# Norm statistics taken while tiles arrive, softmax in PSUM, and a layer loop written out: a two-part network on one core

## The chip, the core and the metric

The kernel runs on one core of a Trainium2 chip. The metric is the device time of one execution in microseconds. Five engines run their own instruction streams and wait for each other through semaphores: PE (matrix multiply; its weight loads are shown apart as PEld), DVE (vector), ACT (activation functions), POOL and SP, which here only issues the weight DMAs. SBUF is the working memory of 128 partitions; PSUM has eight banks of 128 x 512 float32, into which PE writes.

## The reference, cut to what matters

A sequence of 512 tokens of width 1024 goes through two layers of a first kind and then through two layers of a second kind.

```python
# first kind, twice (depth 2)
h = x @ w_in                                    # q, k, v of three attentions, gates
merged = g0*(fox(h)@w_up_fox) + g1*(stick(h)@w_up_sb) + g2*(sparse(h)@w_up_dsa)
x = layer_norm(ALPHA*x + merged @ w_out)        # "norm 1"
ffn = square(relu(x @ w_ff_in)) @ w_ff_out
ple = sigmoid(x @ w_ple_gate) * (p @ w_ple)
x = layer_norm(ALPHA*x + ffn + ple)             # "norm 2"
# layer_norm: (x - mean) * rsqrt(var + eps) * g + b, over the 1024 features

# second kind, twice
h = rms_norm(x); proj = h @ w_in_2
# compressed, selected and windowed attention (8 heads; q and k through rope tables)
pc = softmax(q @ kc + mask);  o_c = pc @ vc     # kc, vc: 31 compressed blocks
# gated linear recurrence: log_a = lam*(1+tanh(..)), a = exp(log_a),
#   h = scan(a, sqrt(1-a^2)*(i*xc))
# convolution branch: GLU, 31 taps, layer norm over 512 features, silu, @ w_pw2
x = x + concat(o*silu(z), h*silu(z), conv*silu(z)) @ w_out
# at the end: rms_norm(x)
```

## The kernel before

Activations lie feature-major: a tile is 128 features x 512 tokens, and x has eight of them (`KT = 8`). All products are done in float32 with three matmuls: every operand is cut into a high and a low part (`x_hi`, `x_lo`, `w_hi`, `w_lo`), and high x high, low x high and high x low are summed in PSUM (lines 397 to 399 in `pe_tile`). A weight unit is 128 x 1024 floats; a dense unit (`pe_unit`) is 8 tiles x 3 = 24 matmuls into one bank. Weights stream through four slots: SP loads `w_raw`, ACT makes `w_hi` (L406, after the slot's former unit was used), POOL makes `w_lo` (L423), and only then can PE use the unit. So each unit costs one ACT and one POOL instruction, and the order in which ACT comes to them is part of its program.

There is no scheduler. Each engine's program is written out by hand, and the order in it is the order of the code; waits are on semaphore counts. `pe_group` runs four units: the first two side by side, tile by tile as `x_ready` counts up (`pe_two_units`), then the others one after the other.

A layer norm of the first kind works in five steps over eight tiles: PE sums the tiles with a matrix of 1/1024 (L796), one tile behind the unit that makes it; when all eight are summed, DVE subtracts the mean (L837); ACT squares each tile (L820, two work tiles in turn) and PE sums the squares (L810); ACT takes the root (L822), DVE the reciprocal (L839); DVE multiplies (L843), ACT writes `x_hi` and a float32 copy with scale and bias (L826), DVE writes `x_lo` (L847), which counts `x_ready`. Behind norm 1, PE runs the two PLE units (four products of `p` each into banks 0 to 3), ACT copies each unit's four banks out (L1155) and then frees them together, and the FFN begins. Behind the very last norm 2, DVE adds `x_hi` and `x_lo` into `residual` (L1928), ACT squares it (L1395), PE sums (L1387), and root (L1400), reciprocal (L1414), scaling (L1418) and the split (L1407, L1423) follow.

Each layer of the second kind runs on DVE in this order: norm, rope tables from the positions (nine instructions, `b_rope_tables`), a small polynomial (`b_softplus`), gates and the 31-tap convolution (L1949 to L1967), the gate of the heads (L1981, on which PE's second rope matmul L1534 waits), rope and the block splits, the log decay (L2028), squares of `a` (L2068), the recurrence's factor (L2071), compressed keys and values into place (L2076, L2082), the scan (L2090), the compressed softmax (L2099 to L2119), the split of the convolution's output (L2122), and the copy of the compressed output (L2129). PE meanwhile runs dense units, the scores of the compressed attention (L1656), two more dense units, then the turned softmax weights (L1667), the product with the compressed values (L1675), two `pw2` units, and then the 64 steps of windowed and selected attention in two halves (`attn_pe`: scores L491, turn L501, output L520).

Both layer kinds are hardware loops over `DEPTH` on every engine, and the two attention halves are a loop too.

Of the kernel before, what the change touches and what calls it, by code (L numbers as in the profile page):

```python
# [24 lines left out]
P = 128  # L25
SEQ = 512
# [76 lines left out]
def plan(nc, ctx):  # L103
# [62 lines left out]
    S.eps = small("ln_eps", 1)  # L166

# [2225 lines left out]
```

## Time and profile before

| | |
|---|---|
| Median of three runs | 3076.24 us (3069.5, 3076.24, 3076.39) |
| Profiled execution | 3074.71 us, span 3072.9 us, mean granted clock 0.96 |
| PE busy | 2834.2 us (92%) |
| PE weight loads | 2209.6 us (72%) |
| DVE, ACT, POOL busy | 1564.3, 1171.7, 1069.9 us |
| DMA | 220.57 MB, mean 72 GB/s |

The span runs from the first to the last instruction. A busy share says how long an engine ran, not whether something waited for it; what counts is the idle time of the engine that bounds the span, and what ended it. The clock is that granted to PE: 1.00 is 2.4 GHz and 0.50 is 1.2 GHz; the mean over a stretch mixes the two.

### The profile page before, as it was taken

Reading aid. Unit: us, or ns where it says so; the run is one execution under the profiler, and the core shown is the slowest. Engines: PE = TensorE matmul, PEld = TensorE weight load, DVE = VectorE, ACT = ScalarE, POOL = GpSimd, SP = SyncE. Lnnn points to the kernel's source line nnn. Section 1 sums busy time; section 2 is a strip of 40 time slices with the busy share of each in tenths; the row PEclk is TensorE's granted clock in tenths of the full one; section 3 lists DMA queues with packets and bytes.
Section 4 is the critical chain, followed back from the end, with each engine's and each line's share of the span. In section 5 each row is a group of like instructions: output and inputs, shape, how many; then the busy total and the mean of one; then the engine's idle time right before and its main releaser. Section 6 shows DMA issues by size and latency. Waiting matters only on the chain. (4 is left out here: it accounts for less than half of the span.)

```text
span 3072.9 us, 39249 instructions
## 1 busy us (share of the span) xinstructions
PE 2834.2 (92%) x12850; PEld 2209.6 (72%) x12860; DVE 1564.3 (51%) x2745; ACT 1171.7 (38%) x1921; POOL 1069.9 (35%) x430
## 2 busy tenths in 40 slices
PE   7989899999999899998998999997996998998798
PEld 6857666678888687676766888865875776876676
DVE  2077536453232304764455223327898555889554
ACT  2344434243222433443424323235344443355343
POOL 3422112344444343111133445442464212455312
PEclk9999999999999999999999999998997999999899
DMA  4311111223233122111121232221231001222101
GB/s 151 102 49 49 37 40 55 76 72 99 90 103 101 59 93 82 36 48 42 36 87 58 94 102 96 96 82 49 98 114 62 28 31 56 96 96 96 35 28 48
DMA packets 61043, 220.57 MB, mean 72 GB/s; under 512 B 6896, under 2 KB 7024, under 8 KB 60784
## 3 DMA queue, kind: packets, MB, share of 16 engines
q1 hardware_dynamic: 60192, 217.12, 21.4%
q10 hardware_dynamic: 720, 1.84, 0.2%
q8 instruction: 66, 1.08, 0.2%
q14 instruction: 65, 0.53, 0.1%
HBM read 216.83 MB, written 2.10 MB: 71 GB/s over the span
## 5 line engine op out<-in xcount | busy, mean ns | idle before, releaser
L423 POOL TENSOR_TENSOR w_lo<-w_raw,w_hi 128x1024 fp32r<-128x1024 f32 x404 | 1018.1, 2528 | 1965.1 <-ACT w_hi L406 1950.7
L397 PE MATMUL bank<-x_hi,w_hi 128*128 128x512 f32 (+1 forms) x2160 | 915.1, 424 | 50.3 <-DVE x_lo L2194 17.7
L398 PE MATMUL bank<-x_lo,w_hi 128*128 128x512 f32 (+1 forms) x2160 | 855.5, 396 | 0.0
L399 PE MATMUL bank<-x_hi,w_lo 128*128 128x512 f32 (+1 forms) x2160 | 854.9, 396 | 0.0
L406 ACT ACTIVATE w_hi<-w_raw 128x1024 fp32r<-128x1024 f32 x400 | 419.3, 1054 | 542.0 <-PE bank L399 527.4
L397 PEld LDWEIGHTS bank<-x_hi,w_hi 128*128 128x128 f32 x2160 | 415.9, 193 | 170.4 <-issue 76.6
L399 PEld LDWEIGHTS bank<-x_hi,w_lo 128*128 128x128 f32 x2160 | 413.6, 191 | 90.1
L398 PEld LDWEIGHTS bank<-x_lo,w_hi 128*128 128x128 f32 x2160 | 416.0, 193 | 86.6 <-issue 13.8
L397 PE MATMUL bank<-rhs_hi,w_hi 128*128 128x512 f32 (+1 forms) x656 | 262.3, 400 | 4.2 <-DVE rhs_lo L1288 4.2
L398 PE MATMUL bank<-rhs_lo,w_hi 128*128 128x512 f32 (+1 forms) x656 | 255.5, 390 | 0.0
L399 PE MATMUL bank<-rhs_hi,w_lo 128*128 128x512 f32 (+1 forms) x656 | 255.3, 389 | 0.0
L543 ACT ACTIVATE work<-bank,neg_max 128x128 f32<-128x128 f32 x216 | 114.0, 528 | 288.5 <-DVE neg_max L564 285.4
L564 DVE TENSOR_REDUCE neg_max<-bank 128x1 f32<-128x128 f32 x216 | 105.3, 490 | 166.3 <-PE bank L491 138.0
L1353 DVE TENSOR_TENSOR ffn_sum<-ffn_sum,bank 128x512 f32 x64 | 43.9, 688 | 286.1 <-PE bank L399 286.1
L1343 DVE TENSOR_TENSOR work<-work 128x512 f32<-128x512 f32 x64 | 102.7, 1604 | 169.5 <-ACT rhs_hi L1170 169.5
L1967 DVE SCALAR_TENSOR_TENSOR bank<-glu_out,params_b_cur,bank 128x512 f32<-128x512 f32 x216 | 152.7, 753 | 34.0 <-issue 34.0
L397 PEld LDWEIGHTS bank<-rhs_hi,w_hi 128*128 128x128 f32 (+1 forms) x656 | 122.9, 187 | 50.9 <-issue 27.8
L1213 DVE TENSOR_SCALAR proj<-proj 128x1024 f32<-128x1024 f32 (+2 forms) x8 | 9.3, 1229 | 267.8 <-ACT proj L1032 267.8
L399 PEld LDWEIGHTS bank<-rhs_hi,w_lo 128*128 128x128 f32 (+1 forms) x656 | 123.0, 188 | 25.9
L398 PEld LDWEIGHTS bank<-rhs_lo,w_hi 128*128 128x128 f32 (+1 forms) x656 | 123.1, 188 | 23.2
L1168 ACT ACTIVATE work<-bank 128x512 f32<-128x512 f32 x64 | 38.0, 594 | 216.4 <-PE bank L399 216.4
L501 PE MATMUL bank<-constants,work 128*128 128x128 f32 x540 | 100.7, 285 | 18.0 <-ACT work L543 17.5
(387 smaller groups left out, 3688.2 us busy)
## 6 DMA issues: line engine op xcount, KB each, us to landing
w_raw<-w SPq DMA_DIRECT2D x404, 512.0 KB, 3.3
ln_in<-x SPq DMA_DIRECT2D x1, 2048.0 KB, 8.1
out<-residual SPq DMA_DIRECT2D x8, 256.0 KB, 2.2
p_raw<-p ACTq DMA_DIRECT2D x2, 512.0 KB, 3.5
positions<-pos ACTq DMA_DIRECT2D x2, 256.0 KB, 3.3
constants<-con SPq DMA_DIRECT2D x1, 455.0 KB, 3.2
cos<-cos SPq DMA_DIRECT2D x1, 256.0 KB, 3.4
sin<-sin SPq DMA_DIRECT2D x1, 256.0 KB, 3.7
```

Source lines behind the costliest of these rows:

```text
L397: nc.tensor.matmul(out, wh, xh, start=first, stop=False)
L398: nc.tensor.matmul(out, wh, xl, start=False, stop=False)
L399: S.last = nc.tensor.matmul(out, wl, xh, start=False, stop=last)
L406: S.nc.scalar.activation(S.wh[s][:, :], S.raw[s][:, :], ACT.Copy).then_inc(S.hi_ready[s], 1)
L423: S.nc.gpsimd.tensor_tensor(S.wl[s][:, :], S.raw[s][:, :], S.wh[s][:, :].bitcast(F32), ALU.subtract).then_inc(S.lo_ready[s], 1)
L501: m = nc.tensor.transpose(o[:, k * P:(k + 1) * P], S.wk[4 + n % 2][:, k * P:(k + 1) * P], ident)
L543: nc.scalar.activation(S.wk[4 + n % 2][:, 0:w], S.X[n % 2][:, 0:w], ACT.Exp, bias=S.nm[n % 4][:, :], accum_out=S.rs[n % 4][:, :]).then_inc ...
L564: nc.vector.tensor_reduce(S.nm[n % 4][:, :], S.X[n % 2][:, 0:w], AX, ALU.max, negate=True).then_inc(Z.max, 1)
L1168: nc.scalar.activation(S.wk[j % 2][:, :], S.ps[s][:, :], ACT.Relu).then_inc(S.bank_free[s], 1)
L1343: nc.vector.tensor_tensor(h, S.wk[j % 2][:, :], S.wk[j % 2][:, :], ALU.mult)
L1353: nc.vector.tensor_tensor(y, y, S.ps[s][:, :], ALU.add).then_inc(S.bank_free[s], 1)
L1967: stt(out=S.X[t % 2][:, :], in0=S.uc[:, bass.ds(i * 3 + (k + t * UC_W), SEQ)], scalar=S.curB[:, bass.ds(i * 3 + (k + PB_DW + t * CONV_K), ...
```

## The change

The norms of the first kind (`ln_*`) subtract twice X[0] from each tile as it comes (X[0] is a 1024th of the sum over the first four tiles, so twice it is their own mean), and square and sum the result at once; tiles 4 to 7 are also summed into X[2], which is the offset that is left. The variance is the sum of squares less the offset squared. The offset is taken out between the multiplications. The last of these norms writes `residual` and its square straight away. The root's table is called for by a dummy activation ahead of it. PLE banks are freed one by one, and the first group behind a norm runs three units side by side.

```diff
+def pe_side_by_side(S, pe, us, g, rh, rl, ready, n0, banks=None, free=None):
+
     for k in range(KT):
         pe.wait_ge(ready, n0 + k + 1)
-        for s in slots:
+        for u in us:
+            s = u % SLOTS
             if k == 0:
                 pe.wait_ge(S.lo_ready[s], g + 1)
                 pe.wait_ge(S.bank_free[s], banks[s] if banks else g + 1)
+                if free:
+                    free(s)
             pe_tile(S, s, k, S.ps[s][:, :], rh, rl, k, k == 0, k == KT - 1)
...
+def pe_group(S, pe, u0, g, rh, rl, ready, n0, banks=None, wide=2, free=None):
+
+    pe_side_by_side(S, pe, range(u0, u0 + wide), g, rh, rl, ready, n0, banks, free)
+    for u in range(u0 + wide, u0 + SLOTS):
...
+def ln_units_pe(S, pe, n0, t_sem, t0, t, unit):
+
+    def first_mean(j):
         pe.wait_ge(t_sem, t0 + j + 1)
-        return S.nc.tensor.matmul(S.X[0][:, :], S.ones[:, :], seq(t, j), start=(j == 0), stop=(j == KT - 1))
-
-    for j in range(SLOTS):
-        unit(j)
-        if 4 * i + j >= 1:
-            mean(4 * i + j - 1)
-    if i == 1:
-        mean(KT - 1).then_inc(S.ln_mean, 1)
-
-
-def ln_pe(S, pe, n0):
-
-    for j in range(KT):
-        pe.wait_ge(S.ln_sq, n0 * KT + j + 1)
-        S.nc.tensor.matmul(S.X[1][:, :], S.ones[:, :], S.wk[j % 2][:, :], start=(j == 0),
-                           stop=(j == KT - 1)).then_inc(S.ln_var, 1)
+        return S.nc.tensor.matmul(S.X[0][:, :], S.ones[:, :], seq(t, j), start=(j == 0), stop=(j == 3))
+
+    for x in range(KT):
+        unit(x)
+        if 1 <= x <= 4:
+            m = first_mean(x - 1)
+            if x == 4:
+                m.then_inc(S.ln_mean, 1)
+        if x == 6:
+            for j in range(4):
+                ln_square_pe(S, pe, n0, j)
+            for j in (4, 5):
+                ln_offset_pe(S, pe, n0, t, j)
+    for j in (4, 5, 6):
+        ln_square_pe(S, pe, n0, j)
+    for j in (6, 7):
+        ln_offset_pe(S, pe, n0, t, j)
+    ln_square_pe(S, pe, n0, 7)
...
+def ln_root_act(S, act, n0, t):
+
+    S.nc.scalar.activation(S.spare[:, :], S.eps[:, :], ACT.Sqrt)
+    ln_square_act(S, act, n0, t, 7)
+    act.wait_ge(S.ln_off, n0 + 1)
+    S.nc.scalar.activation(S.wk[0][:, :], S.X[2][:, :], ACT.Square).then_inc(S.ln_offsq, 1)
+    act.wait_ge(S.ln_v, n0 + 1)
+    S.nc.scalar.activation(S.wk[2][:, :], S.wk[1][:, :], ACT.Sqrt, bias=S.eps[:, :]).then_inc(S.norm_std, 1)
...
+def ln_last_act(S, act, n0, t, g, b):
...
+        S.nc.scalar.activation(S.wk[4 + j % 4][:, :], seq(t, j), ACT.Square, scale=scale, bias=bias).then_inc(S.norm_sq, 1)
+        S.nc.scalar.activation(seq(S.res, j), seq(t, j), ACT.Identity, scale=scale, bias=bias)
...
+def ln_less_first_dve(S, dve, n0, t, x):
+
+    if x == 4:
+        dve.wait_ge(S.ln_mean, n0 + 1)
+    for j in range(0 if x == 4 else x, x + 1):
+        if x >= 4:
+            S.nc.vector.scalar_tensor_tensor(out=seq(t, j), in0=S.X[0][:, :], scalar=-2.0, in1=seq(t, j), op0=ALU.mult,
+                                             op1=ALU.add).then_inc(S.ln_d, 1)
...
+def ln_dve(S, dve, n0, t, last=False):
     nc = S.nc
-    tiles = [t[:, j * SEQ:(j + 1) * SEQ] for j in range(KT)]
-    dve.wait_ge(S.ln_mean, n0 + 1)
-    for j in range(KT):
-        nc.vector.tensor_tensor(tiles[j], tiles[j], S.X[0][:, :], ALU.subtract).then_inc(S.ln_d, 1)
-    dve.wait_ge(S.ln_std, n0 + 1)
-    nc.vector.reciprocal(S.wk[3][:, :], S.wk[2][:, :])
+    tiles = [seq(t, j) for j in range(KT)]
+    dve.wait_ge(S.ln_offsq, n0 + 1)
+    dve.wait_ge(S.norm_var, n0 * KT + KT)
+    nc.vector.tensor_tensor(S.wk[1][:, :], S.X[1][:, :], S.wk[0][:, :], ALU.subtract).then_inc(S.ln_v, 1)
+
+    def center(j):
+        nc.vector.tensor_tensor(tiles[j], tiles[j], S.X[2][:, :], ALU.subtract)
+
+    center(0)
+    dve.wait_ge(S.norm_std, n0 + 1)
+    nc.vector.reciprocal(S.X[3][:, :], S.wk[2][:, :])
     dve.drain()
     for j in range(KT + 2):
         if j < KT:
-            nc.vector.tensor_tensor(tiles[j], tiles[j], S.wk[3][:, :], ALU.mult).then_inc(S.ln_y, 1)
-        if j >= 2:
+            nc.vector.tensor_tensor(tiles[j], tiles[j], S.X[3][:, :], ALU.mult).then_inc(S.norm_y, 1)
+        if j + 1 < KT:
+            center(j + 1)
+        if j >= 2 and not last:
             q = j - 2
-            dve.wait_ge(S.ln_hi, n0 * KT + q + 1)
+            dve.wait_ge(S.norm_hi, n0 * KT + q + 1)
             nc.vector.tensor_tensor(seq(S.xl, q), S.wk[4 + q % 4][:, :], seq(S.xh, q).bitcast(F32),
                                     ALU.subtract).then_inc(S.x_ready, 1)
+        dve.drain()
```

In the last layer of the first kind ACT loads the positions, and DVE makes the rope tables once, between the second and third quarter of the FFN; ACT takes the sines after the third. In the layers of the second kind they are no longer made.

```diff
+        if L == DEPTH - 1:
+            act.dma_start(S.prmB[:, :], T["prm_b"]).then_inc(S.pb_landed, 16)
+            act.dma_start(S.pos[:, :], T["pos"].to_broadcast([P, SEQ])).then_inc(S.pb_landed, 16)
+        with act.Fori(0, 3) as q:
+            ffn(q)
+        if L == DEPTH - 1:
+            act.wait_ge(S.ang_ready, 1)
+            nc.scalar.activation(S.sin[:, :], S.tab[2][:, :], ACT.Sin)
...
+        with dve.Fori(0, 2) as q:
+            ffn(q)
+        if L == DEPTH - 1:
+            b_rope_tables(S, dve)
...
-        b_rope_tables(S, dve, L)
```

The log decay and the squares of `a` go from DVE to ACT, the compressed softmax works in PSUM, the `pw2` units stand ahead of it on PE (their input has its own place, `un_hi` and `un_lo`), and its outputs go to four banks and are copied by two engines. The loops over the layers and over the attention halves are written out on every engine; inside a layer of the first kind the loops over the projections and the FFN stay.

```diff
+        for t in range(4):
+            lam = S.curB[:, PB_LAM + t:PB_LAM + t + 1]
+            nc.scalar.activation(seq(S.la, t), seq(S.la, t), ACT.Identity, scale=lam, bias=lam)
...
+        squared = (S.X[0], S.X[1], S.wk[2], S.wk[3])
+        for t in range(4):
+            nc.scalar.activation(squared[t][:, :], seq(S.la, t), ACT.Square).then_inc(S.a_ready, 1)
+        for t in range(4):
+            nc.scalar.activation(seq(S.unh, t), seq(S.cacc, t), ACT.Copy).then_inc(S.cl_hi, 1)
...
+            nc.vector.tensor_tensor(seq(S.unl, t), seq(S.cacc, t), seq(S.unh, t).bitcast(F32), ALU.subtract).then_inc(S.un_ready, 1)
...
-            p3 = S.wk[4 + h][:, :].rearrange("p (r n) -> p r n", n=32)
-            mx = S.cmx[:, 16 * h:16 * h + 16]
+            p3 = S.X[h][:, :].rearrange("p (r n) -> p r n", n=32)
+            mx = S.cmx[h]
+            nc.vector.tensor_tensor(p4, p4, mask, ALU.add)
...
+        for b in (1, 3):
+            act.wait_ge(S.oc_ready, L * 4 + b + 1)
+            nc.scalar.activation(S.ot2[:, b * 512:(b + 1) * 512], S.X[b][:, :], ACT.Copy).then_inc(S.oc_done, 1)
...
-    with pe.Fori(0, DEPTH) as L:
+    for L in range(DEPTH):
...
-        with pe.Fori(0, 2) as i:
-            pe.wait_ge(S.lru_done, L + 1)
-            pe.wait_ge(S.oc_done, L * 4 + 4)
-            pe.wait_ge(S.mc_y, L * 4 + 4)
+        pe.wait_ge(S.oc_done, L * 4 + 4)
+        for i in range(2):
```

On PE, at the end of norm 1: `merged` is the last output unit, `ln_in` a tile of the norm, `work` a squared tile, `p_hi` the first PLE unit. Before:

```order
L399 MATMUL bank<-merged_hi,w_lo_58 128x512
L796 MATMUL bank<-ln_in,ones 128x512 x2
L809 ISA
L810 MATMUL bank<-work_93,ones 128x512
L809 REGISTER_ALU
L810 MATMUL bank<-work_94,ones 128x512
```

And of the change:

```order
L404 MATMUL bank<-merged_hi,w_lo_58 128x512
L828 MATMUL bank<-work_93,ones 128x512
L828 MATMUL bank<-work_94,ones 128x512
L828 MATMUL bank<-work_95,ones 128x512
L834 MATMUL bank<-ln_in,ones 128x512 x2
L828 MATMUL bank<-work_96,ones 128x512
L402 MATMUL bank<-p_hi,w_hi_55 128x512
```

Behind the last unit there stood one mean matmul and eight squares; now there stand four squares and two offset matmuls, and six of their kind stand between the last two units.

On PE, at the compressed attention: `work` turned are its softmax weights, `un` the convolution's output for `pw2`. Before:

```order
L399 MATMUL bank<-x_hi,w_lo_58 128x512
L1667 MATMUL bank<-constants,work_97 128x128 x4
L1667 MATMUL bank<-constants,work_98 128x128 x4
L1675 MATMUL bank<-cmp_values,work_99 128x256 x4
L1675 MATMUL bank<-cmp_values,work_100 128x256 x4
L1440 REGISTER_ALU
L397 MATMUL bank<-x_hi,w_hi_55 128x512
```

And of the change:

```order
L404 MATMUL bank<-un_hi,w_lo_60 128x512
L1831 MATMUL bank<-constants,work_95 128x128 x4
L1831 MATMUL bank<-constants,work_96 128x128 x4
L1837 MATMUL bank<-cmp_values,work_99 128x256 x4
L1837 MATMUL bank<-cmp_values,work_100 128x256 x4
L496 MATMUL bank<-b_ks,work_93 128x128
```

The two `pw2` units moved ahead of the turned weights; the attention's first scores stand right behind the compressed output.

On DVE, from the factor of the recurrence to the softmax's first half. Before:

```order
L2068 TENSOR_TENSOR work_100<-lru_log_a 128x512
L2071 SCALAR_TENSOR_TENSOR lru_tmp<-work_97,lru_tmp 128x512
L2071 SCALAR_TENSOR_TENSOR lru_tmp<-work_98,lru_tmp 128x512
L2071 SCALAR_TENSOR_TENSOR lru_tmp<-work_99,lru_tmp 128x512
L2071 SCALAR_TENSOR_TENSOR lru_tmp<-work_100,lru_tmp 128x512
L2074 ISA
L2076 COPY cmp_keys<-bank 64x31 x2
L2082 COPY cmp_values<-bank 32x64 x8
L2087 SCALAR_TENSOR_TENSOR lru_i<-lru_i,lru_tmp 128x2048
L2090 TENSOR_TENSOR_SCAN lru_tmp<-lru_log_a,lru_i 128x512 x4
L2099 TENSOR_TENSOR work_97<-bank,cmp_mask 128x512
```

And of the change:

```order
L2194 SCALAR_TENSOR_TENSOR lru_tmp<-bank,lru_tmp 128x512 x2
L2194 SCALAR_TENSOR_TENSOR lru_tmp<-work_95,lru_tmp 128x512
L2194 SCALAR_TENSOR_TENSOR lru_tmp<-work_96,lru_tmp 128x512
L2199 COPY cmp_keys<-bank 64x31 x2
L2205 COPY cmp_values<-bank 32x64 x8
L2210 TENSOR_TENSOR un_lo<-conv_sum,un_hi 128x512 x4
L2214 MEMSET work_93 64x512
L2214 MEMSET work_94 64x512
L2219 SCALAR_TENSOR_TENSOR lru_i<-lru_i,lru_tmp 128x2048
L2222 SCALAR_TENSOR_TENSOR lru_tmp<-lru_log_a,lru_i 128x512 x4
L2231 TENSOR_TENSOR bank<-bank,cmp_mask 128x512
```

The four squares left DVE, the scan's row now reads as L2222, and four subtractions and two memsets that stood behind the softmax came ahead of the scan.

## Rows read from the trace of the kernel before

**Rows 1.** Waits of PE, longest first: total us, times, longest.

```profile
PE bank L1675 <- DVE b_o_tok L2129: 19.3, 2, 9.7
PE bank L1667 <- DVE work L2119: 18.9, 4, 8.9
PE bank L1387 <- ACT work L1395: 18.6, 1, 18.6
PE bank L397 <- ACT ple_proj L1155: 17.6, 4, 4.6
PE bank L501 <- ACT work L543: 17.5, 16, 4.2
PE bank L397 <- DVE x_lo L1423: 16.0, 2, 8.8
...
PE bank L1656 <- DVE cmp_keys L2076: 8.0, 2, 4.0
...
PE bank L1534 <- DVE b_gate_tok L1981: 7.2, 2, 3.6
```

**Rows 2.** Busy time by stretch, with clock: norms, first FFN units, compressed attention.

```profile
core 0: us, PE busy (x) PEld busy (x) DVE busy (x) ACT busy (x) POOL busy (x), PEclk, DMA share, GB/s
594.90:628.70 33.80, 22.65 (x69) 13.01 (x67) 22.13 (x28) 24.60 (x37) 5.13 (x2) 0.94 0.11 39
628.70:653.70 25.00, 24.96 (x97) 20.43 (x98) 16.15 (x7) 7.01 (x10) 10.51 (x4) 0.88 0.19 64
1028.90:1050.80 21.90, 11.38 (x21) 3.52 (x19) 12.44 (x16) 11.00 (x16) 2.86 (x1) 0.86 0.14 47
2058.10:2105.30 47.20, 18.34 (x37) 6.43 (x35) 31.84 (x52) 28.73 (x41) 2.87 (x1) 0.79 0.08 26
2328.80:2397.90 69.10, 42.07 (x160) 34.11 (x159) 49.29 (x56) 21.93 (x30) 31.42 (x11) 0.72 0.15 47
2811.40:2879.40 68.00, 40.96 (x160) 33.20 (x160) 49.28 (x56) 21.94 (x30) 31.40 (x11) 0.76 0.15 48
```

**Rows 3.** PE in order of time, last output unit and norm squares.

```profile
589.91 0.40 PE L399 MATMUL bank<-merged_hi,w_lo 128*128 128x512 f32 x1
...
594.70 0.39 PE L399 MATMUL bank<-merged_hi,w_lo 128*128 128x512 f32 x1
...
599.43 7.70 PE L810 MATMUL bank<-work,ones 128*128 128x512 f32 x16 [1.44 <-ACT work L820]
```

**Rows 4.** DVE in order of time, same norm.

```profile
607.98 3.35 DVE L839 RECIPROCAL work<-work 128x512 f32<-128x512 f32 x1 [5.09 <-ACT work L822]
611.41 1.90 DVE L843 TENSOR_TENSOR ln_in<-ln_in,work 128x512 f32<-128x512 f32 x3
613.69 0.69 DVE L847 TENSOR_TENSOR x_lo<-work,x_hi 128x512 fp32r<-128x512 f32 x1 [0.38 <-ACT work L826]
```

**Rows 5.** ACT in order of time, same norm.

```profile
612.14 0.81 ACT L826 ACTIVATE x_hi<-ln_in,params_cur 128x512 fp32r<-128x512 f32 x1 [4.19 <-DVE ln_in L843]
...
614.98 2.02 ACT L1155 ACTIVATE ple_proj<-bank 128x512 f32<-128x512 f32 x4
```

**Rows 6.** DVE in order of time, start of the second kind of layer.

```profile
2113.22 0.69 DVE L1423 TENSOR_TENSOR x_lo<-work,x_hi 128x512 fp32r<-128x512 f32 x1 [0.16 <-issue]
...
2135.73 0.81 DVE L1961 TENSOR_SCALAR bank<-glu_out,params_b_cur 128x512 f32<-128x512 f32 x1
```

**Rows 7.** ACT in order of time, its fourth unit there.

```profile
2129.36 0.60 ACT L1710 ACTIVATE work<-bank 128x512 f32<-128x512 f32 x1 [3.89 <-PE bank L399]
```

**Rows 8.** DVE by line, 2241 to 2400: count, busy us, mean ns, idle.

```profile
L2028 DVE TENSOR_SCALAR lru_log_a<-lru_log_a,params_b_cur 128x512 f32<-128x512 f32 x4 | 10.2, 2607 | 0.0
...
L2071 DVE SCALAR_TENSOR_TENSOR lru_tmp<-work,lru_tmp 128x512 f32<-128x512 f32 x4 | 8.9, 2278 | 0.1
...
L1990 DVE TENSOR_TENSOR work<-bank,sin 128x512 f32<-128x512 f32 x7 | 4.8, 682 | 3.7 <-PE bank L1534 3.7
```

**Rows 9.** DVE in order of time, between the two halves of windowed attention.

```profile
2472.95 0.62 DVE L564 TENSOR_REDUCE neg_max<-bank 128x1 f32<-128x128 f32 x2 [3.30 <-issue]
```

More of the change, by code:

```diff
@@ L202, in plan @@
     S.X = S.ps[4:]
+    S.cmx, S.csum = ([S.X[3][:, 256 + 32 * n + 16 * h:256 + 32 * n + 16 * h + 16] for h in range(2)] for n in range(2))
     def sem(name):
@@ L816, in ln_act @@
     for j in range(KT):
[L817 to L824 removed]
+        act.wait_ge(S.norm_y, n0 * KT + j + 1)
@@ new lines, in ln_act @@
+        if between:
+            between(j)
+def ln_last_act(S, act, n0, t, g, b):
+    for j in range(KT):
+        act.wait_ge(S.norm_y, n0 * KT + j + 1)
+        if j >= 4:
+            act.wait_ge(S.norm_var, norm(0) * KT + j - 3)
+        scale, bias = S.cur[:, g + j:g + j + 1], S.cur[:, b + j:b + j + 1]
+        S.nc.scalar.activation(S.wk[4 + j % 4][:, :], seq(t, j), ACT.Square, scale=scale, bias=bias).then_inc(S.norm_sq, 1)
+        S.nc.scalar.activation(seq(S.res, j), seq(t, j), ACT.Identity, scale=scale, bias=bias)
@@ L897, in a_tensor @@
     ident = S.con[:, C_ID:C_ID + P]
-    with pe.Fori(0, DEPTH) as L:
+    for L in range(DEPTH):
         G = lambda u, i=0: L * A_GROUPS + u // SLOTS + i
-        with pe.Fori(0, 6) as i:
+        pe_group(S, pe, 0, G(0), S.xh, S.xl, S.x_ready, L * 2 * KT, wide=3 if L else 2)
+        with pe.Fori(1, 6) as i:
             pe_group(S, pe, 0, G(0, i), S.xh, S.xl, S.x_ready, L * 2 * KT)
@@ L1037, in a_scalar @@
         nc.scalar.activation(S.wh[s][:, :], S.raw[s][:, :], ACT.Copy).then_inc(S.hi_ready[s], 1)
-    with act.Fori(0, DEPTH) as L:
+    for L in range(DEPTH):
         G = lambda u, i=0: L * A_GROUPS + u // SLOTS + i
@@ L1475, in nsa_steps @@
                     steps.append(Step(b, qk, v, norm, scale, () if b or e or br == 2 else staged))
+    if i == 0:
+        steps[2].ready += ((S.mc_y, L * 4 + 4),)
     return steps
@@ L1519, in b_tensor @@
         rms_pe(S, pe, 0, j)
-    with pe.Fori(0, DEPTH) as L:
+    for L in range(DEPTH):
         def dense(u):
@@ L1848, in b_scalar @@
             nc.scalar.activation(seq(S.xh, 4 + t), seq(S.zc, t), ACT.Copy).then_inc(S.mc_hi, 1)
-        with act.Fori(0, 2) as i:
+        for i in range(2):
             attn_act(S, act, S.nsa, L * 64 + i * 32, nsa_steps(S, L, i),
@@ L1924, in b_vector @@
     stt = nc.vector.scalar_tensor_tensor
-    dve.drain()
-    for j in range(KT):
-        nc.vector.tensor_tensor(seq(S.res, j), seq(S.xh, j).bitcast(F32), seq(S.xl, j).bitcast(F32),
-                                ALU.add).then_inc(S.res_ready, 1)
-    dve.wait_ge(S.pb_landed, 16)
-    with dve.Fori(0, DEPTH) as L:
+    for L in range(DEPTH):
         nc.vector.tensor_copy(S.curB[:, :], cols(S.prmB, L, PB_N))
@@ L2064, in b_vector @@
         split_hidden(1, 0)
[L2066 removed]
         for t in range(4):
[L2068 to L2071 removed]
+            dve.wait_ge(S.a_ready, L * 4 + t + 1)
+            m = stt(out=seq(S.lrt, t), in0=(S.X[0], S.X[1], S.wk[2], S.wk[3])[t][:, :], scalar=1.0, in1=seq(S.lrt, t), op0=ALU.add, op1=ALU.mult)
         m.then_inc(S.b2_ready, 1)
@@ L2138, in b_vector @@
             free_bank(S, dve, u)
-        with dve.Fori(0, 2) as i:
+        for b in (0, 2):
+            dve.wait_ge(S.oc_ready, L * 4 + b + 1)
+            nc.vector.tensor_copy(S.ot2[:, b * 512:(b + 1) * 512], S.X[b][:, :]).then_inc(S.oc_done, 1)
+        zero_halves(1)
+        for i in range(2):
             attn_dve(S, dve, S.nsa, L * 64 + i * 32, nsa_steps(S, L, i),
```

404 lines of the change are left out of this document (213 added, 191 removed).

## The prediction

> **What bounds the kernel now.** I read the waits of PE first, since PE is busy for 92% of the span. Behind its waits stand the norms of the first kind (the waits on L1395, on L1155 and on L1423) and one place in the second kind, the compressed attention: the waits for L2129, L2119 and L2076 sum to 46.2 us [rows 1]. Then I read stretches with their clock. A norm 1 keeps PE from the last output unit to the first FFN unit for 33.8 us; a norm 2 takes 21.9 us between layers and 47.2 us in front of the second kind; the compressed attention, from the wait for its keys to the first turned weights of the next attention, 69.1 and 68.0 us, in which PE is busy for only 42.1 and 41.0 us at a mean clock of 0.72 and 0.76 [rows 2]. So a wait costs twice: its length, and the work near it that runs at 1.2 GHz instead of 2.4. At the high level 21 matmuls take 594.70 - 589.91 = 4.79 us, 0.228 each, so a unit of 24 takes 5.5 us; a statistics matmul takes at most 7.70/8 = 0.96, I use 0.9 [rows 3].
>
> **Norm 1, twice.** Let E be the end of the last output unit. Of 16 statistics matmuls, seven stood ahead of E and nine behind it; now ten ahead and six behind. So the unit itself ends 3 x 0.9 = 2.7 us later, at E' = E + 2.7. Behind E' PE runs six, 5.4 us. The last square needs DVE's two additions and one subtraction (3 x 0.69 and two short drains) and ACT's square, 0.6: 3.4 us, so PE is the later of the two. Then the variance on DVE (0.7), the root (0.7, its table fetched early) and the reciprocal (3.35 [rows 4]) end at E' + 10.4. DVE does three instructions per tile now instead of two: at 0.61 from start to start (1.90 for three, the last one's tail in it [rows 4]) and a drain that is 2.0 us per tile, against 1.41 on ACT (two of L826). The first `x_lo` lands at E' + 15.0. ACT also copies eight PLE banks at 0.5 each (2.02 for four [rows 5]) and makes two weight splits; the last tile is ready at E' + 27.7.
>
> PE starts PLE at E' + 5.3 and is through with it at E' + 16.3, where before it waited twice for the block copies (17.6 us in four waits [rows 1]). Then three FFN units side by side take 8 x 9 x 0.228 = 16.4 us, less than 1 us delayed by the second PLE unit's banks, and the fourth 5.5: done at E' + 39.1. Ahead of the next group stands a new wait: three units end together, ACT needs 2.3 us for each and POOL 2.8, so the second slot's weights are ready 1.7 us late. That makes E + 43.5 for four units. Before it was 33.8 + 25.0 = 58.8 [rows 2], with the first of them at a low clock. The gain is 15.3, in the second layer about 13.7, as PE's restart there was shorter: 29.
>
> **Norm 2.** The same chain gives the first `x_lo` at E' + 15.0 = E + 17.7 instead of 21.9 [rows 2]. But the tiles then come at DVE's 2.0 us instead of 1.4, and PE has stood idle for 9.6 us and restarts at the low clock, so of 4.2 us I keep 2. Three units wide costs nothing here, since 9 x 0.228 = 2.05 is the pace of the tiles.
>
> In front of the second kind the residual's eight additions and its eight squares behind them are gone: ACT writes square and residual at 1.4 per tile from E' + 11.2, the last square is summed by E' + 23.5 (this matmul at the low clock), the root ends at 24.3, and from the reciprocal's start to PE's first matmul I take 6.5 as now: E' + 30.8 = E + 33.5 against 47.2 [rows 2]. Gain 13.7.
>
> **Rope tables and the gate wait, twice.** From the last `x_lo` to the convolution's first instruction DVE takes 2135.73 - 2113.22 = 22.5 us [rows 6]. Without tables the fourth unit's copy ends this stretch, at 2129.36 + 0.60 [rows 7] plus 0.7 for the gate: DVE is 5.0 us earlier. PE's wait for the gate is 3.6 per layer [rows 1]; it goes, and with it low-clock work worth 2.3: 11.8 for both. Next after it DVE is 1.4 us ahead. The tables' nine instructions now stand in the FFN, where DVE has 10.9 us until the next pair of units ends; uncovered they would cost up to 12, and I take 0.
>
> **Compressed attention, twice.** On DVE the log decay (10.2) and the squares (5.7 in the same view) go, and the factor (8.9 for four, under POOL's splits, 2.28 each [rows 8]) comes while POOL is idle, 0.7 each. The keys are in place 10 us earlier, so the 4.0 wait of L1656 goes. ACT's eight additions take 5 us ahead of its Silu work and cost PE 0.4. Four subtractions and two memsets come ahead of the scan, two of the subtractions at the long price, and the softmax starts about where it did against PE's scores. Its chain is 4.8 us to the exponentials and 4.8 after them. It ran into POOL's 14 us of products before; in PSUM it should not, since instructions with one operand there keep their 0.68 us (mean over seven [rows 8]). PE, from the keys on: scores 3.5 to 4.5, two dense units 11, two `pw2` units 11, so it comes to the softmax's weights 26 us after the keys, when the chain is through by a hair. Then the turn 1.1, ACT's copy 0.9, products 3.9, their last copy and the staging of q 2.0. There the attention opens, but ACT still has two splits, four copies and a table load (5.6 us) before the first exponential, now bare. Sum: 27 + 1.1 + 0.9 + 3.9 + 2.0 + 5.0 = 39.9 with 27 the upper end; I take 39.3, against 69.1 and 68.0 [rows 2]: gain 58.5.
>
> The Trainium skill, SBUF — State Buffer, section SBUF: two separate sides, says that a vector instruction with at most one SBUF input, outside the two-port modes, does not contend with GpSimd, and one with two does. By that rule the softmax is free of POOL and the moved subtractions are not, as in my sum; the 0.68 mean agrees.
>
> **Between the attention halves, and the rest.** DVE stands 3.30 us with no releaser at the loop's turn [rows 9], and PE 4.2 [rows 1]. Written out, what is left is row maximum and exponential, 1.2: two times 3.0 plus 1.5 of low clock, 9. At the layer boundary the root is 1.4 us earlier. What the longer code costs: nothing in straight stretches, where the rows show no such stop; the lower end is a gain of 3.3 at each of two other turns, the upper 3.3 at as many new places as there are.
>
> The Trainium skill, Runtime: NRT & Kernel Launch, Instruction fetch mechanics, holds that straight code is fetched ahead and that a taken branch out of the window stalls. By it unrolling only gains, as I have it; [rows 9] agree.
>
> Sum: 29 + 2 + 13.7 + 11.8 + 58.5 + 9 + 1.4 = 125. The profiled execution took 3074.7 us (1.8 of it outside the span), the median of the runs 3076.2, 1.5 more: 3074.7 - 125 = 2949.7, and 2951 for the median.
>
> **Rivals.** (1) The chains in the second kind are longer than PE's cover. The softmax starts behind scan and subtractions; if all four subtractions meet POOL (4 x 1.6 us more) and ACT's staging comes late, each layer loses 10, and the gate wait keeps half of its low-clock share: 2951 + 24 = 2975. For it: two engines finish within 1 us of each other in my sum. Against it: PE's two `pw2` units are 11 us of cover that was not there.
> (2) The gains are larger: all PE work runs at 2.4 GHz once the waits are gone, the other turns gain 3.3 each. By the skill's fetch rule as well: 2951 - 16 = 2935.
> (3) The norms do not gain: the banks and weight slots behind three units side by side make PE wait at each group, and DVE's third instruction sets the pace. Half of the norms' 45 goes: 2973.
> (4) Slower than before: the code written out (DVE's rows go from 1206 to 2231, PE's from 3123 to 6844) makes PE run out of instructions. The price is the 3.30 us of [rows 9] at each refill; it decides from 38 refills on PE's path, and at 43 gives 3092. Against it: the attention's 32 steps are straight code now and show no such stop.
> (5) The change does not do what it says, the waits only move: 3070.
>
> **How the numbers follow.** My forecast 0.56, rival 1 0.16, rival 2 0.13, rival 3 0.10, rival 4 0.02, rival 5 0.03. The likeliest gives 2951, from 2938 to 2966 by its own unknowns: 12 for the tables, 8 for the exponential's start, 6 for scores and clock. The range for 8 in 10 reaches into rivals 1 to 3: 2930 to 2982. 0.3% (9 us) is about what a measurement here can tell from no change: faster 0.96, same 0.02, slower 0.02.
>
> **What would show it.** The wait for L2129 gone, that for L2119's successor under 2 us; no wait of the rope matmul on the gate; the clock of the compressed stretch above 0.9; the stretch from the last output unit to the fourth FFN unit 43 us; the first matmul of the second kind 33 us behind the last gate unit; a wait of 4 to 5 us at the attention's first turn, of about 1 between its halves. It is wrong if DVE's softmax ends more than 2 us behind the second `pw2` unit, if PE waits for weights behind three wide units for more than 3 us, or if idle time without a releaser appears on PE.

## The result, and the profile after

| | before | changed |
|---|---|---|
| Median | 3076.31 us (4 runs, 3069.5 to 3077.2) | 2948.05 us (4 runs, 2946.75 to 2949.31) |
| Ratio, 95% interval | | 0.9592 (0.9581 to 0.9604) |
| Span of the profiled execution | 3072.9 us | 2947.0 us |
| PE busy / mean granted clock | 2834.2 us / 0.96 | 2793.0 us / 0.978 |

2951 was forecast. PE computes the same 9168 product matmuls in both kernels, so the end of the n-th of them is a ruler: where the changed kernel reaches it earlier, time has been saved. Between the places named below the two traces stay at the same distance to 0.02 us through whole FFNs; only inside the attentions of the first kind do they wander, by up to 3 us, with the same code.

| Stretch | forecast, us | saved by the ruler, us |
|---|---|---|
| norm 1, both layers | 29 | 14.4 + 12.9 = 27.3 |
| norm 2 between the layers | 2 | 3.0 |
| norm 2 in front of the second kind | 13.7 | 14.1 |
| rope tables and gate wait, both layers | 11.8 | 6.4 + 5.2 - 1.1 - 1.1 = 9.4 |
| compressed attention, both layers | 58.5 | 28.8 + 27.6 = 56.4 |
| between the attention halves | 9 | 5.7 + 5.4 = 11.1 |
| layer boundary | 1.4 | 4.0 |
| elsewhere | 0 | 0.6 |
| sum | 125 | 125.9 |

Three rows fall short of the forecast, by 6.2 us together, and the others exceed it by 6.7: that the sum fits so closely is partly luck.

First the waits of PE in the changed kernel; the columns are those of [rows 1].

```profile
PE bank L402 <- DVE x_lo L2323: 17.0, 2, 16.6
PE bank L506 <- ACT work L548: 16.5, 17, 4.8
PE bank L402 <- DVE x_lo L1576: 14.2, 2, 7.1
...
PE bank L402 <- DVE x_lo L910: 12.5, 5, 9.7
...
PE bank L1540 <- ACT work L874: 7.2, 3, 6.6
...
PE bank L496 <- issue: 3.8, 2, 1.9
...
PE bank L402 <- ACT silu_z_nsa L1866: 2.7, 2, 1.4
PE bank L1837 <- ACT work L1983: 1.5, 2, 0.7
```

Five of the eight rows of [rows 1] have no long successor: the waits for the compressed output (19.3), for its weights (18.9), for the PLE copies (17.6), for the keys (8.0) and for the gate (7.2) are gone. A sixth, the wait for the residual's squares (18.6), has shrunk to the 7.2 of L1540. L506 is the attention's turn: its longest wait, 4.8, is the first exponential's. A small row is new, L1866, one unit's silu on ACT; the prediction did not have it. The row of L496 names no releaser, which the prediction gave as a sign of being wrong. It is no stop of PE's own: ACT's staging of q ends at 2312.91, and PE's first scores start at 2313.01; the kernel before waits 1.9 us at the same place. The first row is the load of the input at the start, as before.

Then the stretches of [rows 2]. The last output unit ends at 597.43, the last unit in front of norm 2 at 1016.95, the last one before the second kind at 2030.70, and the scores of the compressed attention begin at 2278.60; the first turned weights of the attention come at 2318.84.

```profile
597.40:614.40 17.00, 16.14 (x62) 11.01 (x60) 13.27 (x14) 10.54 (x16) 4.80 (x2) 1.00 0.10 31
614.40:638.10 23.70, 23.14 (x99) 18.30 (x99) 22.62 (x20) 14.11 (x21) 7.25 (x3) 1.00 0.18 62
1016.90:1031.80 14.90, 5.21 (x14) 1.99 (x12) 11.18 (x13) 8.93 (x13) 2.34 (x1) 0.83 0.11 35
2030.70:2060.60 29.90, 15.51 (x29) 5.53 (x28) 23.31 (x38) 18.93 (x27) 2.34 (x1) 0.83 0.05 18
2278.60:2318.80 40.20, 31.87 (x159) 26.01 (x157) 27.30 (x40) 17.97 (x27) 28.18 (x10) 0.93 0.23 75
```

Read beside [rows 2]: behind norm 1 PE is busy for 39.3 of 40.7 us at full clock, where it had 47.6 of 58.8. A norm 2 still leaves it idle, at a mean clock of 0.83. The compressed attention takes 40.2 us in both layers, where it took 69.1 and 68.0.

### The profile page after: what moved, and what is told of

The parts are those of the page before. It is cut to its first block and busy times, and to the rows that moved or that the text cites. A ratio compares the mean times of both kernels' runs of the same rounds, so it can differ in the third digit from the quotient of the medians.

```text
span 2947.0 us, 37005 instructions
## 1 busy us (share of the span) xinstructions
PE 2793.0 (95%) x12850; PEld 2185.3 (74%) x12860; DVE 1504.0 (51%) x2736; ACT 1149.8 (39%) x1915; POOL 1059.3 (36%) x430
## 5 line engine op out<-in xcount | busy, mean ns | idle before, releaser
L402 PE MATMUL bank<-x_hi,w_hi 128*128 128x512 f32 x2128 | 895.1, 421 | 47.4 <-DVE x_lo L2323 17.0
L404 PE MATMUL bank<-x_hi,w_lo 128*128 128x512 f32 x2128 | 838.2, 394 | 0.0
L403 PE MATMUL bank<-x_lo,w_hi 128*128 128x512 f32 x2128 | 837.4, 394 | 0.0
L402 PEld LDWEIGHTS bank<-x_hi,w_hi 128*128 128x128 f32 x2128 | 406.0, 191 | 166.3 <-issue 56.2
L404 PEld LDWEIGHTS bank<-x_hi,w_lo 128*128 128x128 f32 x2128 | 404.3, 190 | 87.7
L403 PEld LDWEIGHTS bank<-x_lo,w_hi 128*128 128x128 f32 x2128 | 406.5, 191 | 83.1 <-issue 12.7
L1483 DVE TENSOR_TENSOR work<-work 128x512 f32<-128x512 f32 x64 | 93.8, 1465 | 135.3 <-ACT rhs_hi L1262 135.3
L402 PEld LDWEIGHTS bank<-rhs_hi,w_hi 128*128 128x128 f32 (+1 forms) x656 | 122.9, 187 | 50.8 <-issue 27.7
L506 PE MATMUL bank<-constants,work 128*128 128x128 f32 x540 | 100.0, 284 | 16.9 <-ACT work L548 16.5
```

What stands on the lines that cost most here:

```text
L402: nc.tensor.matmul(out, wh, xh, start=first, stop=False)
L403: nc.tensor.matmul(out, wh, xl, start=False, stop=False)
L404: S.last = nc.tensor.matmul(out, wl, xh, start=False, stop=last)
L506: m = nc.tensor.transpose(o[:, k * P:(k + 1) * P], S.wk[4 + n % 2][:, k * P:(k + 1) * P], ident)
L1483: nc.vector.tensor_tensor(h, S.wk[j % 2][:, :], S.wk[j % 2][:, :], ALU.mult)
```

## The experiments

Each kernel was timed beside the kernel before, and the ratios are to that; "by the ruler" is the distance of its trace from that of the kernel it was made from, over the stretches that the edit touches.

### The compressed softmax in SBUF again

```diff
-            p3 = S.X[h][:, :].rearrange("p (r n) -> p r n", n=32)
-            mx = S.cmx[h]
-            nc.vector.tensor_tensor(p4, p4, mask, ALU.add)
+            p3 = S.wk[2 + h][:, :].rearrange("p (r n) -> p r n", n=32)
+            mx = S.cm[:, 16 * h:16 * h + 16]
+            nc.vector.tensor_tensor(p4, S.X[h][...], mask, ALU.add)
```

(shortened; the exponential and the sum move to the same work tiles and to SBUF likewise.)

> The changed kernel with its compressed softmax in SBUF again (scores come from the bank, everything behind them works in two work tiles, maximum and sum in SBUF). In the changed kernel the softmax takes DVE from 2292.4 to 2301.7 while POOL runs three products of 4.6 us each, and PE comes for the weights at 2305.6, 3.9 us later. My theory (place decides): at least two of the instructions, one in each part behind the first exponential, now wait 3 to 4 us for POOL, as L2112 (3.74) and L2117 (4.06) did in the kernel before; the chain ends 8 us later, PE waits 4 us per layer and works another 1 at 1.2 GHz: 2958 us (2953 to 2970). Rival (place is nothing, the short times come from the moment at which the softmax now runs): all instructions stay at 0.7 us and less, 2948.

Measured: 2974.58 us, ratio 0.9684 (0.9669 to 0.9699); by the ruler 14.3 and 14.1 us lost. The rival is out, and my own figure was too small. DVE in order of time, changed kernel first, then this one, and under it POOL at that time:

```profile
2293.16 0.70 DVE L2233 TENSOR_REDUCE bank<-bank 128x16 f32<-128x512 f32 x1
...
2293.93 0.17 DVE L2236 TENSOR_SCALAR cmp_norm<-bank 128x16 f32<-128x16 f32 x1
...
2294.18 0.70 DVE L2238 TENSOR_TENSOR bank<-bank,cmp_norm 128x512 f32<-128x512 f32 x1
```

```profile
2293.12 0.69 DVE L2233 TENSOR_REDUCE cmp_norm<-work 128x16 f32<-128x512 f32 x1
2293.88 4.14 DVE L2236 TENSOR_SCALAR cmp_norm<-cmp_norm 128x16 f32<-128x16 f32 x1
2298.10 4.91 DVE L2238 TENSOR_TENSOR work<-work,cmp_norm 128x512 f32<-128x512 f32 x1
...
2303.69 0.69 DVE L2233 TENSOR_REDUCE cmp_norm<-work 128x16 f32<-128x512 f32 x1
...
2311.71 0.69 DVE L2254 TENSOR_TENSOR work<-work,cmp_norm 128x512 f32<-128x512 f32 x1
```

```profile
2293.38 4.61 POOL L458 TENSOR_TENSOR x_hi<-lru_tmp,silu_z_lru 128x2048 fp32r<-128x2048 f32 x1 [9.68 <-PE bank L404]
2297.94 4.52 POOL L459 TENSOR_TENSOR lru_log_a<-lru_tmp,silu_z_lru 128x2048 f32<-128x2048 f32 x1
2302.60 4.77 POOL L461 TENSOR_TENSOR x_lo<-lru_log_a,x_hi 128x2048 fp32r<-128x2048 f32 x1
```

Sixteen columns take 0.17 us with their operand in a bank and 4.14 in SBUF: the instruction ends 0.03 us behind POOL's product, the next one 0.5 behind the following product. The reduction at 2303.69, with one SBUF operand and in the middle of a product, keeps its 0.69. The multiplication at 2311.71 has two SBUF operands like that of L2238, and takes 0.69 while POOL is idle: so it takes both, the place and POOL. The chain ends 15.0 us later (2316.7, not 2301.7), and PE pays for it at a place I had not looked at:

```profile
PE bank L402 <- ACT silu_z_nsa L1866: 28.7, 2, 14.4
```

ACT's program has the last silu behind the exponentials. Late exponentials hold it up, and the second `pw2` unit cannot start: PE's wait for that silu is 14.4 us, where it was 1.4. So the cover of two units that I counted is broken by a queue, not by the weights.

### The pw2 units behind the compressed output again

```diff
-        for u in (B_PW2, B_PW2 + 1):
-            pairs_pe(S, pe, L, u, S.unh, S.unl, 0, S.un_ready, L * 4)
...
+        for u in (B_PW2, B_PW2 + 1):
+            pairs_pe(S, pe, L, u, S.unh, S.unl, 0, S.un_ready, L * 4)
         pe.wait_ge(S.oc_done, L * 4 + 4)
```

(now behind the products with the values; DVE's two copies of the output move ahead of its `pw2` additions.)

> The changed kernel with the two pw2 units on PE behind the compressed output again (DVE and ACT in that order too; the turned weights go to other work tiles, for the sake of the tiles that pw2 still reads). Theory (the cover is what pays, the shorter chain pays the rest): PE comes for the weights 12.5 us earlier, at 2293.1, and they are there at 2299.5 and 2301.7: 8.6 us of waiting, 1 more for ACT's copies, 2 of work at 1.2 GHz, less 1.9 for the output's copies, now hidden: 9 to 10 per layer, 2967 us (2960 to 2974). Rival (the gain came from the shorter DVE and ACT chains alone, the order is worth nothing): 2948 to 2952. Third (the order is all of it): 27 per layer back, 3002.

Measured: 2960.92 us, ratio 0.9644 (0.9629 to 0.9659); by the ruler 7.4 and 6.0 lost, where 9 to 10 were expected. Of the 7.4, 1.1 comes 150 us later, from the clock alone, behind waits of equal length. In the two stretches PE's idle time grows by 7.5 us, the rest is low clock. The order is worth 12 to 13 of the 56 us: both single-cause theories fall. The other 43 are what is left over, for the softmax in PSUM and the shorter DVE and ACT chains together. By the run before, 28 us hang on the softmax's place; the decay and the squares on ACT were not tried by themselves.

```profile
PE bank L506 <- ACT work L548: 15.4, 16, 4.2
PE bank L1828 <- DVE work L2254: 14.8, 4, 6.3
```

### Two units side by side instead of three

```diff
-        ffn_in(0, 0, 3)
+        ffn_in(0, 0, 2)
```

(and likewise for the first projections of the second layer.)

> The changed kernel with two units side by side behind each norm of the first kind, as before, not three. Theory: DVE gives a tile every 2.0 us and two units take 1.37 of it. Norm 1: the PLE units keep PE busy while the tiles come, so only about 1 us each. Norm 2 between the layers: 0.6 x 8 = 5 us. Sum 6: 2954 us (2950 to 2958). Rival (three wide costs as much as it saves, by the second slot's weights that come late): 2947.

Measured: 2950.5 us, ratio 0.9611 (0.9598 to 0.9624), not told apart from the changed kernel by the times. By the ruler 1.9 is lost at each norm 1 and 0.1 at norm 2. There my 5 us were wrong: from the first matmul to the end of the 96th it takes 24.58 us here and 24.49 in the changed kernel. I had counted 0.6 us of waiting for each of eight tiles. But PE restarts at the low clock with 0.43 us from one matmul's start to the next, so six of them take longer than the 2.0 us in which a tile comes, and PE waits for the fourth and the fifth tile only, 0.8 us in all. The last three tiles are ready 1.4, 0.8 and 0.9 us apart, and PE needs 1.4 for each. PE in order of time, behind norm 2 of this kernel:

```profile
1037.94 0.79 PE L402 MATMUL bank<-x_hi,w_hi 128*128 128x512 f32 x1 [9.68 <-DVE x_lo L910]
...
1040.24 0.63 PE L404 MATMUL bank<-x_hi,w_lo 128*128 128x512 f32 x1
...
1043.88 0.50 PE L402 MATMUL bank<-x_hi,w_hi 128*128 128x512 f32 x1
...
1045.86 0.50 PE L402 MATMUL bank<-x_hi,w_hi 128*128 128x512 f32 x1 [0.32 <-DVE x_lo L910]
```

The comparison is not quite even: 7 matmuls ran at the low clock here and 11 in the changed kernel, which is worth 0.8 us. What two units would lose behind 11 was not measured.

### Another order on ACT

```diff
+        z(B_ZN, S.zn, 3)
         for h in range(2):
             act.wait_ge(S.cexp_in, L * 2 + h + 1)
             nc.scalar.activation(S.X[h][:, :], S.X[h][:, :], ACT.Exp).then_inc(S.cexp_out, 1)
-        z(B_ZN, S.zn, 3)
...
         nsa_stage(0, 0)
         used(L, B_PW2)
+        mc_copy(0)
+        mc_copy(1)
...
-                     lambda n: nsa_after(n, i))
+                     lambda n: nsa_after(n, i), None if i else lambda: (mc_copy(2), mc_copy(3)))
```

(shortened: the staging, the split and the first two copies now stand ahead of ACT's copies of the turned weights and of the compressed output; copies 2 and 3 stand behind the attention's first exponentials.)

> The changed kernel with ACT's order around the compressed softmax changed: the last silu(z) ahead of the exponentials (PE waits 1.36 us for it between the pw2 units), the first staging of q and the first pw2 slot's split in the stretch where ACT is idle, the last two copies behind the attention's first exponentials. Theory: the waits in front of the first scores (1.90), between the pw2 units (1.36) and at the first turn (4.4 to 4.8, of which 1.2 stay) go: 6.5 per layer, 2935 us (2931 to 2940). Rival (the next wait stands right behind: row maximum, POOL's splits of the out units' weights): 2 to 3 per layer, 2943.

Measured: 2926.46 us (2925.63 to 2930.82), ratio 0.953 (0.9517 to 0.9543): faster than both kernels. The changed kernel's ACT at the first turn, and then this one's:

```profile
2312.94 2.00 ACT L411 ACTIVATE w_hi<-w_raw 128x1024 fp32r<-128x1024 f32 x2
2314.85 2.17 ACT L2007 ACTIVATE x_hi<-silu_z_conv 128x512 fp32r<-128x512 f32 x4
2317.04 1.28 ACT L548 ACT_TABLE_LOAD   x1
2318.33 0.37 ACT L548 ACTIVATE work<-bank,neg_max 128x128 f32<-128x128 f32 x1
```

```profile
2312.72 0.60 ACT L2012 ACTIVATE b_o_tok<-bank 128x512 f32<-128x512 f32 x1 [1.13 <-PE bank L1839]
2314.27 0.37 ACT L548 ACTIVATE work<-bank,neg_max 128x128 f32<-128x128 f32 x1 [0.96 <-DVE neg_max L571]
```

ACT now waits for the row maximum with its table in place. In the two stretches PE's idle time falls by 13.6 us (8.4 to 1.8 and 8.7 to 1.8), as expected (13); the time falls by 19.3 by the ruler (9.6 and 9.7). The difference, 5.7, is the clock, which my figure did not have. This stretch and the attention half behind it, and the same half in the changed kernel:

```profile
2281.80:2315.80 34.00, 32.24 (x165) 26.68 (x164) 27.59 (x41) 15.42 (x25) 24.18 (x8) 1.00 0.18 62
```

```profile
2315.80:2386.40 70.60, 69.45 (x437) 55.74 (x436) 43.83 (x153) 32.94 (x90) 18.41 (x10) 1.00 0.14 46
```

```profile
2318.80:2392.80 74.00, 72.81 (x440) 57.77 (x441) 44.14 (x154) 32.72 (x90) 14.33 (x8) 0.97 0.09 32
```

### The attention halves written out, alone

```diff
-        with dve.Fori(0, 2) as i:
+        for i in range(2):
             attn_dve(S, dve, S.nsa, L * 64 + i * 32, nsa_steps(S, L, i), ...
```

(the same on PE and ACT, in the kernel before.) In the first of the two runs the second half's q came from the first half's columns, so its output differs; the second run has its own.

> The kernel before with one edit: the loop over the two attention halves is written out on PE, ACT and DVE. Theory (DVE's 3.30 us is the loop's turn): it goes in both layers, with some low clock behind it: 3.3 to 5 per layer, 3068 us (3066 to 3071). Rival 1 (the stop belongs to the work at this place): 3076. Rival 2 (code written out costs refills): above 3078.

> The kernel before with the two attention halves written out, and nothing else (in the run halves_written_out the second half's q was staged from the first half's columns; here each half has its own). Theory: the same instructions and waits, so the same time: 12 us less than before, a ratio of 0.996 (0.994 to 0.998); DVE's 3.30 us at the turn is gone, PE's wait there is 1.0. Rival (that time depended on the data): 0.998 or more.

Measured: 3059.94 us, ratio 0.9957 (0.9941 to 0.9973), and 3056.46 us, ratio 0.995 (0.9932 to 0.9968): the first was more than expected, the second as expected, and the rivals are out. By the ruler each layer gains 6.7 to 7. DVE goes through the place without a stop, where [rows 9] show 3.30 us:

```profile
2464.02 0.68 DVE L1504 TENSOR_TENSOR residual<-residual,bank 128x512 f32<-128x512 f32 x1
2464.86 0.62 DVE L564 TENSOR_REDUCE neg_max<-bank 128x1 f32<-128x128 f32 x2 [0.16 <-PE bank L491]
```

PE's wait shrinks by only 3.1 us per turn. Again the clock has the rest: the second half, which begins at the turn, and the stretch behind it, in the kernel before and in the second run:

```profile
2476.50:2549.00 72.50, 69.88 (x438) 56.23 (x437) 45.50 (x155) 33.60 (x88) 9.54 (x4) 0.99 0.08 26
2549.00:2589.00 40.00, 31.18 (x114) 22.32 (x113) 14.51 (x33) 12.50 (x18) 9.55 (x4) 0.89 0.18 61
```

```profile
2467.20:2538.80 71.60, 69.08 (x437) 55.78 (x437) 45.68 (x156) 33.82 (x88) 9.53 (x4) 1.00 0.11 34
2538.80:2577.40 38.60, 29.47 (x113) 21.07 (x113) 14.42 (x32) 12.48 (x18) 9.54 (x4) 0.93 0.19 63
```

So the gain has two parts. At the turn and up to the end of the half it is 5.2 us, 3.1 of waiting and 2.1 of clock. The other 1.6 comes only 75 us later, behind PE's wait for the attention's output, whose length is the same in all kernels, 2.0 us. There the clock either stays high or falls for 7 or 8 matmuls. Both happen in one trace, that of the changed kernel, in its two layers:

```profile
2463.83 0.47 PE L402 MATMUL bank<-nsa_hi,w_hi 128*128 128x512 f32 x1 [1.96 <-DVE nsa_lo L2279]
2464.14 0.40 PE L403 MATMUL bank<-nsa_lo,w_hi 128*128 128x512 f32 x1
```

```profile
2903.96 0.68 PE L402 MATMUL bank<-nsa_hi,w_hi 128*128 128x512 f32 x1 [1.96 <-DVE nsa_lo L2279]
2904.44 0.63 PE L403 MATMUL bank<-nsa_lo,w_hi 128*128 128x512 f32 x1
```

It falls in 4 of 4 cases in the two traces whose halves are a loop, and in 5 of 20 where they are written out. How much of this 1.6 is the edit's is therefore open.

### All layer loops written out too

The same edit on the loops over `DEPTH`, on every engine (with the first run's q).

> The kernel before with the attention halves and all loops over the layers written out on every engine. Theory: to the 8 us of the halves come one turn of the layer loop in each kind, where PE waits for DVE: 2 to 4 in the second kind (its wait at the boundary was 8.8, in the changed kernel 7.1), up to 3 in the first: 3064 us (3061 to 3068). Rival (four more long stretches of code cost refills, 3.3 each): 3069 to 3085.

Measured: 3053.94 us, ratio 0.9939 (0.9922 to 0.9955); the trace has PE's wait at the layer boundary at 7.1 instead of 8.8, and no new idle place. What went is a stop of ACT ahead of the root's table, here in the kernel before and in this one:

```profile
2579.75 1.28 ACT L1400 ACT_TABLE_LOAD   x1 [1.85 <-issue]
```

```profile
2571.20 1.28 ACT L1400 ACT_TABLE_LOAD   x1
```

By the ruler the boundary gives 2.5. Code written out costs nothing on PE's path here; rival 4 is out. That the layer loops bring more than the halves alone can't be said from the times: the intervals overlap, and part of the difference is not the loops'. Behind norm 1 it has the instructions, order and waits of the kernel before, and yet another clock over the same 96 product matmuls, here first in this kernel, then in the kernel before:

```profile
621.30:650.50 29.20, 25.03 (x97) 20.11 (x97) 18.83 (x14) 16.05 (x25) 8.54 (x4) 0.88 0.10 36
```

```profile
617.60:648.40 30.80, 26.51 (x98) 21.16 (x97) 18.89 (x15) 16.00 (x25) 8.41 (x4) 0.83 0.10 35
```

The difference is 1.6 us. How long the low clock lasts behind one and the same wait differs by that much from run to run.

### The rope tables in each layer again

```diff
         rms_dve(S, dve, L)
+        b_rope_tables(S, dve, L)
```

(and no longer in the FFN.)

> The changed kernel with the rope tables made in each layer of the second kind again, by the nine DVE instructions behind the norm, and no longer in the FFN. Theory: the gate waits come back, 3.6 and 2.1 to 2.8 of work at 1.2 GHz per layer, 5 to 6.4: 2959.5 us (2957 to 2963). If the instructions in the FFN had cost something there, it would come off. Rival (what gained at this place was the unrolled code, not the tables): 2948.

Measured: 2963.67 us, ratio 0.9643 (0.9623 to 0.9662); by the ruler 6.3 and 7.1 lost. PE waits for the gate again, for 3.6 and 5.7 us:

```profile
PE bank L1663 <- DVE b_gate_tok L2109: 9.2, 2, 5.7
```

Nothing came back from the FFN: there the two traces keep their distance, so the nine instructions were free at that place, as costed.

### Without the dummy root

```diff
-    S.nc.scalar.activation(S.spare[:, :], S.eps[:, :], ACT.Sqrt)
```

> The changed kernel without the dummy root that calls for the table ahead of the last square. Theory: a table load of 1.28 us comes onto the chain of each of the four norms; in the two norms 1 PE has other work (PLE units) and loses under 1, in the two norms 2 it loses all of it: 3 to 4 us in the span, and the waits for the norm 2 (9.7 and 6.6) are 1.3 longer. Rival (the load is taken at the same moment anyway, while ACT waits for the offset): no difference.

Measured: 2950.18 us in one run; by the ruler within 0.3 us at every norm, and the waits at norm 2 are 9.7 and 6.6 as before. The rival was right. ACT in order of time at norm 1:

```profile
604.82 0.60 ACT L850 ACTIVATE work<-bank 128x512 f32<-128x512 f32 x1 [1.37 <-PE bank L834]
605.43 1.28 ACT L852 ACT_TABLE_LOAD   x1
606.73 0.72 ACT L852 ACTIVATE work<-work,ln_eps 128x512 f32<-128x512 f32 x1
```

The load falls into the time in which ACT waits for the variance anyway.

### The norms alone

The changed kernel with the second kind as before; of the second kind's edits only POOL's loop over the layers stays written out.

> The changed kernel with the whole second kind as before (rope tables per layer, decay and squares on DVE, softmax in SBUF, pw2 behind, its loops as hardware loops): only the norms, the PLE banks, three units side by side and the written-out loops of the first kind are left of the change. Theory (the parts add up, since each ends at a place where PE is the one that is waited for): in the changed kernel PE is 45.0 us ahead where the second kind's first four units are done; nothing is added behind it: 45 less than the kernel before, 3031 us against 3076 (3027 to 3036), a ratio of 0.985. Rival (the second kind's gains needed the earlier work, or the 45 us are paid back in its waits): under 35 or over 55.

Measured: 3034.61 us, ratio 0.9872 (0.9849 to 0.9894), so 39.3 us gained, not 45. The norms of the first kind give what they gave (by the ruler 14.4, 3.2 and 12.9). The 5.7 that are missing have three places. With its hardware loop over the layers the second kind starts 2.0 later (PE's wait there is 8.2, not 7.1). Then, since PE is early and DVE still makes the tables, the gate costs 1.8 and 3.0 more than in the kernel before, of which later stretches of the first of these layers give 4.1 back. The rest, 3.9 in the profiled execution, lies in the attentions of the first kind, which wander.

```profile
PE bank L1654 <- DVE b_gate_tok L2094: 8.9, 2, 4.5
```

What of the first norm's gain belongs to the PLE banks and what to the statistics, no run separates.

So the parts add up within their intervals, save for what DVE, second in line, takes back where only PE has become earlier.

## Why the prediction was right, and where it was off

**Norm 1.** Right by its steps. The first tile was forecast at E' + 15.0, and the last one ready at E' + 27.7: the last `x_lo` ends at 626.49, E' + 29.1. PLE ends at E' + 16.1 (16.3). The first tile came at E' + 16.9, since DVE's first `x_lo` took 2.78 us beside POOL; PE paid 0.86. E' itself is 3.4 behind E, not 2.7 (E is 594.04 here: the end in the trace before, 595.09, less the 1.05 by which this one was already ahead). The wait for weights behind three wide units was 0.4, not 1.7. The four units end at E + 44.1 with the next wait still to come (43.5 with it); the gain fell short by 1.7 over both layers. Rival 3 is out.

**Norm 2.** The first tile came at E' + 14.8 (15.0) and from E (2058.2 less the 30.9 already saved) to the second kind's first matmul it took 33.3 (33.5). Between the layers 3.0 were saved (2). The third unit side by side, which I had called free, is indeed free here, and it brought nothing; behind norm 1 it brought 1.9 each.

**Tables and gate.** The wait went and 11.6 us with it, as forecast (11.8). What I missed is a new wait of 0.8 per layer for a weight's low part on POOL, once PE comes earlier, which with its clock cost 1.1 each.

**Compressed attention.** The forecast had 39.3 from the keys to the first turn, measured 40.2. Three of DVE's four subtractions for `un_lo` met POOL, not two, and the four took 9.6 us, which is rival 1's price. Yet the softmax ended at 2301.7 and PE came at 2305.6: 3.9 us of room, where I had "by a hair". The wait for the silu (1.36) was not in my sum. With the last copy and the staging of q, 2.0 in the sum, I was right: PE waited 1.90. From the first scores to the first turned weights it took 5.8, not 5.0; the bare wait itself was right, 4.4 and 4.8 against "4 to 5". The total gain is 2.1 below the forecast.

**Halves and boundary.** The mechanism was right (DVE's 3.30 is the loop's turn), the size too small: 11.1 and 4.0 against 9 and 1.4. The term mis-sized at the turns is the low clock: 1.5 per turn in the sum, 2.4 per turn measured here (11.1 less 6.3 of waiting, over two). At the boundary PE's wait fell by 1.7 (1.4), and the run with all loops written out has the same 7.1. So this is the turn of the layer loop, where ACT stood 1.85 us, and none of it is owed to another edit. The rest of the 4.0 is clock, which I had left at nothing: 0.7 right behind that wait, and 1.6 behind the wait of 2.0 us ahead of it, where the clock falls or stays as told above. That 1.6 is luck as far as the runs show.

**The rest of the rivals.** Rival 2 had the other turns and a higher clock: part of it came, in the terms for the halves and the boundary. Rivals 4 and 5 are out.

The rule of the Trainium skill, SBUF — State Buffer, section SBUF: two separate sides, held for the softmax: L2238 took 0.70 us with one SBUF input and 4.91 with two, each beside a POOL product. The instruction on 16 columns, 0.17 with its input in PSUM and 4.14 in SBUF, has one SBUF input, and the rule would have it contend only in a two-port mode; whether it runs in one, no run here shows. The rule on instruction fetch (Runtime: NRT & Kernel Launch, Instruction fetch mechanics, in the Trainium skill) agrees with the runs that changed nothing but the loops: DVE's stop of 3.30 us at the turn went. That the stop is a fetch, no run here shows.

## What to carry to other kernels

Price a wait by its length and by the clock behind it: here 13.6 us of waits removed gave 19.3, and each of two turns with 3.1 of waiting gave 5.2. Before two units are counted as cover, follow what else is queued behind the late result on every engine that must free something for them. When PE is 95% busy, look for what stands ahead of the one result that PE waits for: here moving a few copies, a silu and a table load on ACT was worth 19.3 us, while nine DVE instructions put into the FFN cost nothing.

## What was unexpected of the hardware

The low level of PE's clock behind an equal wait lasts unequally long: the same 96 matmuls took 1.65 us more in one run than in another, and behind one and the same wait of 2.0 us the clock fell for 7 or 8 matmuls in 9 of 24 cases and not at all in the others. A DVE instruction on 16 columns took 4.14 us in SBUF beside a POOL product, 24 times its 0.17 us, while a reduction of 512 columns from SBUF in the middle of such a product kept 0.69. What decides between the two was not tried.
